# A mixture-of-experts step on one core: row gathers and transposes of 128 slots in place of 72 to 96

## What is computed

```
def hier_route(x2d, ...):            # top-1 of 4 expert groups, then top-2 of its 8 experts
    ...
    return eidx, gates               # 2 experts and 2 gates for each of the 1088 tokens

def moe_ffn(x2d, eidx, gates, w1, w3, w2):
    ...
    def expert_block(args):
        xb, e = args
        h = jax.nn.silu(xb @ w1[e]) * (xb @ w3[e])
        return h @ w2[e]
    ...
    return jax.ops.segment_sum(out[dest] * g_sorted[:, None], tok, num_segments=T)
```

## Time and profile before

| | |
|---|---|
| median of 3 runs | 1025.65 us (1024.0 to 1025.76) |
| the profiled execution, its time | 1025.95 us |
| its span, first to last instruction | 1024.3 us |
| PE busy | 900.9 us (88%) |
| DVE, ACT, POOL busy | 253.3, 107.3, 157.4 us |
| DMA | 258.21 MB, mean 252 GB/s |
| queue of SP (weights and the rest) | 238.54 MB, 60.6% of 16 engines |
| queue of POOL (gathers, scatters) | 18.95 MB, 8.1% of 16 engines |

### The profile page before, as it was taken

One profiled execution on the slowest core, in us unless ns is written; L12 is line 12 of the kernel. 1 busy time (PEld: TensorE's weight loads), 2 busy tenths in 40 slices (PEclk: granted clock), 3 DMA queues, 4 the chain that ended last, 5 costly groups with the idle time before them and its releaser, 6 DMA issues. The chain is left out here.

```text
span 1024.3 us, 24975 instructions
## 1 busy us (share of the span) xinstructions
PE 900.9 (88%) x10522; PEld 582.3 (57%) x10522; DVE 253.3 (25%) x769; ACT 107.3 (10%) x172; POOL 157.4 (15%) x239
## 2 busy tenths in 40 slices
PE   5999999999999973999999879889887999897950
PEld 2545545455455542777677747557565675674630
DVE  1434452454534553410101100100000000000006
ACT  0211110111101110001000001000010010010014
POOL 1000000000000002112131312122122122112210
PEclk9999999999999995999999999999999999998985
DMA  9760010100101162999999999999999999999828
GB/s 345 278 245 21 22 41 0 41 21 21 41 0 43 42 250 102 387 370 387 367 381 354 376 362 385 360 380 377 372 380 373 385 384 370 361 389 361 319 67 324
DMA packets 57934, 258.21 MB, mean 252 GB/s; under 512 B 11409, under 2 KB 12489, under 8 KB 40852
## 3 DMA queue, kind: packets, MB, share of 16 engines
q1 hardware_dynamic: 47740, 238.54, 60.6%
q0 software_dynamic: 10144, 18.95, 8.1%
HBM read 234.55 MB, written 24.60 MB: 253 GB/s over the span
## 5 line engine op out<-in xcount | busy, mean ns | idle before, releaser
L1204 PEld LDWEIGHTS ps<-hT,big 128*64 128x64 f32 x8192 | 289.7, 139 | 55.4 <-issue 32.3
L1204 PE MATMUL ps<-hT,big 128*64 128x64 f32 (+8 forms) x8192 | 301.2, 234 | 21.9 <-DMA big<-in_exp_w 12.5
L1221 PE MATMUL ps<-big,poolT 128*64 128x512 f32 (+8 forms) x512 | 203.0, 619 | 23.8 <-DMA big<-in_exp_w 18.6
L1101 PE MATMUL ps<-big,hT 128*128 128x512 f32 x384 | 169.4, 600 | 3.5 <-DMA big<-in_w_in 2.2
L1221 PEld LDWEIGHTS ps<-big,poolT 128*64 128x64 f32 (+8 forms) x512 | 64.8, 151 | 135.7 <-issue 111.8
L1101 PEld LDWEIGHTS ps<-big,hT 128*128 128x128 f32 x384 | 73.1, 192 | 94.5 <-issue 88.4
L997 DVE TENSOR_TENSOR poolT<-u,ps 128x256 f32<-128x256 f32 (+8 forms) x32 | 15.1, 471 | 446.2 <-PE ps L1204 389.9
L551 POOL DMA_INDIRECT x_rows<-xn,sidx x32 | 49.4, 1545 | 385.3 <-ACT xn L707 264.1
L531 POOL DMA_INDIRECT slot_table<-ids,dest x18 | 18.7, 1038 | 328.2 <-DVE dest L819 271.9
L707 ACT ACTIVATE xn<-ps,gslot 96x1024 f32<-96x1024 f32 (+6 forms) x23 | 25.5, 1110 | 339.2 <-DMA gslot<-gate_rows,pidx 194.8
L1158 PE MATMUL ps<-big,yT 128*128 128x512 f32 x128 | 56.4, 593 | 0.9 <-DVE yT L886 0.9
(11 more groups left out here) (170 smaller groups left out, 481.9 us busy)
## 6 DMA issues: line engine op xcount, KB each, us to landing
big<-in_exp_w SPq DMA_DIRECT2D x192, 1024.0 KB, 26.5
big<-in_w_in SPq DMA_DIRECT2D x4, 1536.0 KB, 13.2
big<-in_w_out SPq DMA_DIRECT2D x2, 2048.0 KB, 14.9
x_rows<-xres SPq DMA_DIRECT2D x8, 512.0 KB
h_rows<-xn SPq DMA_DIRECT2D x8, 512.0 KB, 2.7
big<-x_rows SPq DMA_DIRECT2D x8, 512.0 KB, 7.1
out_y_prompt<-big SPq DMA_DIRECT2D x8, 512.0 KB, 3.0
xres<-in_x_prompt SPq DMA_DIRECT2D x1, 3072.0 KB, 11.1
```

The lines of the kernel that those rows point to most:

```text
L1101: last = pe.matmul(ps[0:m, bank, :], hT[:, k, 0:m], win[:, k, part * AW:(part + 1) * AW], start=(k == 0), stop=(k == KD - 1))
L1204: last = pe.matmul(out[c * w:(c + 1) * w, j, 0:m], up_weights(n)[:, k, j * P + c * w:j * P + (c + 1) * w], xT[:, 4 * half + k, 0:m], start ...
L1221: last = pe.matmul(ps[first:first + m, 5 + cols, :], hhT[:, 2 * half + k, 0:m], down_weights(n)[:, k, cols * 512:(cols + 1) * 512], start= ...
```

## The change

The load of `tabs` takes 128 ranks instead of 96. `fetch` has no number of slots any more: the index copy and the gather always have 128 slots, rank r from and to partition r. Slots that no token takes are skipped as before. The transposes of a block's rows have always 128 rows. The constant `SMALL` goes. How many slots are computed, gated and added back stays as it was, with the classes.

```diff
-SMALL = max(c[1] for _, _, c in CLASSES)
...
-            sp.dma_start(tabs.rearrange("p e c -> p (e c)")[0:CAP, :],
-                         slot_table.rearrange("(r e) c -> r (e c)", e=NE)[0:CAP, :]).then_inc(tabs_in, 16)
+            sp.dma_start(tabs.rearrange("p e c -> p (e c)"),
+                         slot_table.rearrange("(r e) c -> r (e c)", e=NE)[0:P, :]).then_inc(tabs_in, 16)
...
-            def fetch(b, s, e, m):
+            def fetch(b, s, e):
 
-                pool.tensor_copy(gidx[s][0:m, :], entries(e, m, 0)).then_inc(gidx_ready, 1)
+                token = tabs[:, e, 0:1] if isinstance(e, int) else tabs[:, bass.ds(e, 1), 0]
+                pool.tensor_copy(gidx[s][:, :], token).then_inc(gidx_ready, 1)
...
-                gather(xg[s][0:m, :], gidx[s][0:m, :], rows_in[s])
+                gather(xg[s][:, :], gidx[s][:, :], rows_in[s])
...
-                        fetch(b + 2, s, after[s], SMALL if s else m)
+                        fetch(b + 2, s, after[s])
...
-                fetch(s, s, FIRST + s, CAP)
+                fetch(s, s, FIRST + s)
...
-                        turn(xg[1 - s], max(caps_of[1 - s], SMALL), xgT_done)
+                        turn(xg[1 - s], P, xgT_done)
...
-            turn(xg[0], CAP, xgT_done)
+            turn(xg[0], P, xgT_done)
```

## The result

| | before | after |
|---|---|---|
| median of 4 runs each | 1024.92 us | 1011.15 us (1009.28 to 1015.34) |
| ratio | | 0.9872, 95% interval 0.9837 to 0.9906 |
| the profiled execution, its time and span | 1025.95, 1024.3 us | 1015.34, 1013.7 us |

The forecast was 1040 us, with 0.84 on slower. The profiled execution of after is the slowest of its four runs, so its trace shows a little less than the whole gain.

A forecast was written before the change was run, and what follows sets the result against it. The prediction took the weight stream on the DMA engines as the bound, its slowest engine setting the end. All terms were 0 except uneven gather rows, between +9 and +17, taken as +14: 1025.95 + 14 = 1040 us, range 1027 to 1052.

The forecast's parts named there:

- What the gather moves: the same rows: Expert gathers: empty slots moved nothing before either and each assignment is gathered once, 68 rows a gather; 0.
- What bounds the kernel: Expert part: the weight stream sets the end; the slowest DMA engine ends 8.0 us behind the mean, with PE waiting.
- Each engine has its own rate, 26 GB/s: Weight stream at 940 us: 420 GB/s at share 1.03, so engines mostly run at their own rate, 4 KB in 0.16 us.
- Unevenness, taken as +14: Gathers' rows on the DMA engines: first engines get 8 rows of every gather, 17 us of extra work; taken as +14 us.
- Table and index copies, 0: Table load before the first gather, 32 KB instead of 24 KB, and POOL's index copies of 128 partitions: 0.
- Transposes, 0: PE's transposes of 128 rows: eight take 1.05 us against 1.11 us for eight of 72, so 0.
- The bound of 8 x 50 ns a turn in the rival: PE's 31 turns on the path: longer transposes cost at most 12 us if proportional to columns; no chance of its own.
- Faster: Gathers: 76-slot ones leave their 4 engines and filled slots fall on all 16; about 4 us off, 1022 us; chance 0.08.
- Everything meets: Scatters and gathers load the same first engines: 17 + 15 - 8 = +24, 1050 us; chance 0.12.
- Common limit: DMA engines: their sum binds, loaded engines speed up when others rest, same bytes; 0, 1026 us; chance 0.08.
- the rule on divisors: Row transfers: a DMA takes the largest number of engines up to 16 dividing its outer size; 72 take 12, 76 take 4.
- The signs to look for: Later windows and drain: right if share falls below 1.02, PE waits longer for weights, drain misses 20 us and more.

The follow-up runs named there:

- e4: The changed kernel with 96 slots in the index copy and gather of every block, transposes of 128: 1039.02 us, ratio 1.0144.
- e3: The changed kernel with 112 slots in the index copy and gather of every block, transposes of 128: 1039.25 us, ratio 1.0140.
- e1: The changed kernel with the transposes of the kernel before (72 to 96 rows), gathers of 128 slots: 1012.05 us, ratio 0.9857.
- e2: The kernel before with the transposes of the change (128 rows), gathers as before: 1024.52 us, ratio 1.0001.
- e6: The changed kernel with each scatter's rows rounded up to a multiple of 16, gathers left alone: 1000.90 us, ratio 0.9764.
- e11: The changed kernel with 96 slots for the larger expert of each pair and 128 for the smaller: 1023.65 us, ratio 0.9992.
- e8: The changed kernel with the first of each expert's six weight chunks loaded as two transfers of 64 partitions: 1229.34 us, ratio 1.1989.
- e10: The changed kernel with each gather of 128 slots split into two of 64, to the lower and upper partitions: 1041.71 us, ratio 1.0151.

## Why the prediction was wrong

The step that failed is the term "What the gather moves: the same rows", put at 0. Behind it stands the sentence "there is a common slow-down now and then", which took the dip to 322 GB/s at full share for something that comes and goes whatever the gathers do. But that window, 954 to 958 us, lies 6.6 to 10.6 us behind the last gather of 72 slots:

```profile
947.36 1.05 POOL L541 DMA_INDIRECT xg<-h_rows,gidx  x1 [0.87 <-POOL gidx L566]
```

The runs showed a hold-up of the stream behind each of the 29 short gathers, 25 to 28 us in all, and a gather of 128 slots doesn't have it.

- **What bounds the kernel**: right over the stretch from 440 to 940 us, where the rate of the stream moved the time. "PE is there at once" is not what the trace of before says at the end: the 0.66 us of idle time ahead of the last product are not put down to weights, and PE had waited for none since 935.32 us. PE and the last weights arrived within 1 us of each other, and that was read as a wait. In after PE does wait there, 3.47 us.
- **Each engine has its own rate, 26 GB/s**: right for a stretch without a hold-up (420 GB/s), and 324 GB/s for 5 us behind each gather. The views to see it were at hand: the windows of the earlier trace rows have shares of 1.02 and 1.03 with 377 and 371 GB/s, where another stretch has 420. A missing tenth at full share had to be asked about, gather by gather.
- **"The same rows" move, hence 0 for what the gather moves**: the rows' own transfer is indeed the same. That a gather costs others something was never priced. This missing term is -25 to -27 us by the windows, -28 by e4 against after.
- **Unevenness, taken as +14**: the size was right, in part by luck, since 14 was chosen between 9 and 17. With hold-ups as before (the table's rows of before and e4) and all slots side by side, e3 and e4 take 14 us more than before. e4 moves as much as before up to 940 us (185.8 MB against 186.6), so nearly all of its loss comes behind that. From 8.0 us the drain grew to 16.5 in after, where I had expected 20 and more, and the later windows lose share. What the 14 us consist of is less sure than their size: dealing the ranks gives 5.7 us (some 9 by the estimate above), rounding up the scatters 10.3, and both together 16.6, about the sum. That the gathers' rows and the four-engine scatters meet on the same engines is argued.
- **Table and index copies, 0**: no run has them alone; e1, which has them with the gather, gives the whole gain. The index copies take 0.18 us in one half of a pair and 0.75 in the other, with 88 and 72 slots before as with 128 after, so their size doesn't show.
- **Transposes, 0**: right (e2: 1.0001). The bound of 8 x 50 ns a turn in the rival was too low for a cost in proportion to the columns (from 72 to 128 it would be 0.86 us a turn, 27 us in all), but as the earlier trace rows said, there is no such cost.
- **The sum**: with the missing term it would be +14 - 28 = -14, and -13.8 was measured (1024.92 to 1011.15). This is no check, because both terms are differences of the same run, e4, and must add up to it. With the 25 to 27 us of the windows in place of the 28 it is -11 to -13.
- **The rivals**: "Faster" had the sign and the wrong reason. It rested on slots dealt in turn, for which the traces give no sign: the landing of the slowest gather went from 19.1 us to 17.8 us only. e6, which changes only the scatters, brings the slowest to 10.3 us, so the late gathers were held up by the scatters. "Everything meets" (+24) is not what e3 and e4 show: with the hold-ups left in they came to +14. Its 15 us for the scatters had no working. "Common limit" asked whether engines share a limit, and answered with another stretch's 420 GB/s; both are true, at different times. It did not ask what switches between them.
- **Readings of rows**: of the rule on divisors the rows bear out 76 and 72 rows, none shows 128. The two windows of the second gather hold 73 of its 76 rows. The 9 tenths of the earlier trace rows run from 410 to 947 us, the slice behind that has 8. None of this changes the sum.
- **The signs to look for**: two signs of being right came (PE waits longer for weights from 560 to 1000 us, 41.7 us against 31.1, and a longer drain) in a kernel that was faster. "Share stays and the time is up" and "share stays and the time is as before" were listed; "share stays, rate and speed up" was not. The share had to be read together with the GB/s.

Shown by runs: the gain lies in the gathers (e1, e2), only at 128 of the sizes tried (e3, e4), gather by gather (e11). Argued: that the hold-up is a meeting of engines at SBUF's ports. e8 and e10 agree with it, and neither looks at the hold-up's inside. Where the dip 1 to 5 us behind every gather comes from, what draws it out behind a short one, and why two gathers of 64 don't spread better, stays open.

## What to carry to other kernels

Beside a stream that fills the DMA engines, give an indirect gather into SBUF 128 slots even if most are skipped; each shorter one, of 72 slots or of 112, cost the stream 0.8 to 1.0 us here (0.78 in e11, 0.93 in before, 28 us for 29 gathers in e3), and no line of the profile names it as the cause. Where the DMA share is full, read the GB/s beside it, and if it lies below the best stretch, line the dips up with the transfers issued a few microseconds earlier, over all of them and not only a few. Then level the engines: deal filled slots over the partitions and give scatters a multiple of 16 rows (here 16.6 us for both).

## What was not expected of the hardware

- Behind a gather of 72 to 112 slots the stream runs at 321 to 334 GB/s in the mean from 5 to 9 us after the issue, behind one of 128 at 399, while the share of busy DMA time is the same (1.02 to 1.03 from 5 to 10 us).
- Around every gather, whatever its size, the rate falls to some 350 GB/s from 1 to 5 us after its issue, where the 4 us ahead of it have 408 to 415.
- A sixth of the weights (32 chunks of 1 MB) in transfers of 64 partitions costs 211 us against the same bytes in transfers of 128 (1229.34 and 1018.35 us). Half the rate for these 33.6 MB alone would be some 70 us more (149 us at 225 GB/s, 80 us at 420), so other chunks seem to be held back too.
- Two transfers of half the columns in place of one cost 7 us over the whole kernel (1018.35, two runs, against 1011.15; 32 chunks of 192), though every one still spans all partitions.
